# The end of the mix of a hybrid decoder layer: out gate by Tanh in block portions, norms of the linear group split by token halves

## What is computed

```python
x = x + 0.5 * swiglu(rmsnorm(x, g1), w_gate1, w_up1, w_down1)
h = rmsnorm(x, mix_norm)
sq, sk, sv, gq, gk, gv, gg, glr, mq = split(h @ w_in)
y_swa = swa_attention(sq, sk, sv, ...)        # sliding window of 128, 8 heads: 4 tiles of 128 rows
y_gla = gla(gq, gk, gv, gg, glr, ...)         # linear attention, 4 heads of 64: 2 tiles
#   inside: o = rmsnorm(o, norm_gain)  per head;  return o * silu(out_gate)
y_mem = memory_attention(mq, mk, mv, ...)     # cross attention into 256 memory tokens: 2 tiles
x = x + concat(y_swa, y_gla, y_mem) @ w_out
x = x + 0.5 * swiglu(rmsnorm(x, g2), w_gate2, w_up2, w_down2)
```

## Time and profile before

| | us |
|---|---|
| median of 3 runs | 1776.75 (1771.37 to 1780.1) |
| the profiled execution, its own time | 1777.78 |
| span of that execution in the trace | 1776.0 |
| mean granted TensorE clock in it | 0.988 of full |
| PE busy | 97% |
| DVE busy | 63% |
| ACT busy | 41% |
| POOL busy | 30% |

### The profile page before, as it was taken

How to read it: one execution, slowest core, us unless ns; L and a number is a source line. 1 busy time by engine, 2 the same in 40 slices (tenths; PEclk the granted TensorE clock), 3 DMA queues, 4 the chain that set the end, 5 groups by cost and what they waited for, 6 DMA issues and landing times.

```text
span 1776.0 us, 24794 instructions
## 1 busy us (share of the span) xinstructions
PE 1714.7 (97%) x8295; PEld 1389.5 (78%) x8295; DVE 1127.0 (63%) x1573; ACT 719.9 (41%) x1344; POOL 528.6 (30%) x432
## 2 busy tenths in 40 slices
PE   7999999999999999999999789999999999999999
PEld 4888888888778789877666568688888888877877
DVE  8965565555498684358788662896555555549654
ACT  5533333334234552142167721443333333334432
POOL 0444554443130231000056512044455444310000
PEclk9999999999999999999989989999999999999999
DMA  7142223324944330120100122113222332493334
GB/s 197 66 153 95 94 94 114 123 100 148 357 141 114 111 121 17 70 72 14 36 1 2 37 96 89 65 46 139 101 89 103 123 116 89 166 361 107 95 95 160
DMA packets 101693, 191.69 MB, mean 108 GB/s; under 512 B 11491, under 2 KB 13972, under 8 KB 101612
## 3 DMA queue, kind: packets, MB, share of 16 engines
q1 hardware_dynamic: 100528, 188.48, 31.3%
q0 software_dynamic: 848, 2.10, 0.9%
q10 hardware_dynamic: 236, 0.06, 0.0%
HBM read 139.74 MB, written 50.86 MB: 107 GB/s over the span
## 4 chain that ended last, share of the span: by engine, by line
PE 88%; DVE 3%; DMA 3%; ACT 2%; issue 1%; POOL 1%; SPq 1%; DVEq 0%; ACTq 0%; POOLq 0%
PE ps L56 27%; PE ps L57 27%; PE ps L58 27%; DMA down_raw<-act_dram 3%; PE ps L1565 1%; PE ps L1256 1%; POOL Pg L1883 1%; PE ps L1536 1%; ACT glu L1694 1%; DVE ps L1267 1%; PE ps L1517 1%; PE ps L2230 0%; SPq L971 0%; DVE p_lo L1188 0%; PE ps L1614 0%
## 5 line engine op out<-in xcount | busy, mean ns | idle before, releaser
L474 DVE TENSOR_TENSOR ring<-w_raw,ring 128x512 fp32r<-128x512 f32 x240 | 235.8, 997 | 220.2 <-ACT ring L469 220.0
L56 PE MATMUL ps<-hiT,ring 128*128 128x512 f32 x672 | 261.5, 389 | 0.0
L58 PE MATMUL ps<-hiT,ring 128*128 128x512 f32 x672 | 261.4, 389 | 0.0
L56 PE MATMUL ps<-down_ring 128*128 128x512 f32 x616 | 241.8, 392 | 11.2 <-DVE down_ring L847 6.9
L57 PE MATMUL ps<-loT,ring 128*128 128x512 f32 x640 | 249.0, 389 | 0.0
L57 PE MATMUL ps<-down_ring 128*128 128x512 f32 x616 | 239.9, 389 | 0.0
L58 PE MATMUL ps<-down_ring 128*128 128x512 f32 x616 | 239.8, 389 | 0.0
L56 PE MATMUL ps<-hiB,ring 128*128 128x512 f32 x576 | 225.7, 392 | 4.4 <-DVE loB L360 4.3
L58 PE MATMUL ps<-hiB,ring 128*128 128x512 f32 x576 | 224.6, 390 | 0.0
L469 ACT ACTIVATE ring<-w_raw 128x512 fp32r<-128x512 f32 x240 | 150.3, 628 | 175.7 <-PE ps L58 163.6
L847 DVE TENSOR_TENSOR down_ring<-down_raw,down_ring 128x512 fp32r<-128x512 f32 x176 | 126.4, 729 | 124.2 <-ACT down_ring L843 123.9
(11 more groups left out here) (242 smaller groups left out, 3020.2 us busy)
## 6 DMA issues: line engine op xcount, KB each, us to landing
down_raw<-act_dram SPq DMA_DIRECT2D x154, 256.0 KB, 2.6
w_raw<-in_w_gate SPq DMA_DIRECT2D x88, 256.0 KB, 3.1
w_raw<-in_w_up SPq DMA_DIRECT2D x88, 256.0 KB, 3.2
act_dram<-actT SPq DMA_DIRECT2D x88, 256.0 KB, 2.0
wd<-in_w_down SPq DMA_DIRECT2D x88, 256.0 KB, 5.4
act_dram<-act SPq DMA_DIRECT2D x66, 256.0 KB, 2.0
p_raw<-in_w_proj SPq DMA_DIRECT2D x15, 512.0 KB, 3.5
xT<-in_x SPq DMA_DIRECT2D x8, 512.0 KB, 7.4
```

The lines of the kernel that those rows point to most:

```text
L56: nc.tensor.matmul(out, w_hi, x_hi, start=first, stop=False, skip_group_check=resumed)
L58: return nc.tensor.matmul(out, w_lo, x_hi, start=False, stop=last, skip_group_check=resumed)
L474: nc.vector.tensor_tensor(ring[:, e % RING, 1, :], op_source(e), ring[:, e % RING, 0, :].bitcast(F32), ALU.subtract).then_inc(op_ready, 1)
```

## The change

In `mix_*` and `out_*`:

- The gate silu(z) = z * sigmoid(z) is computed as 0.5 * z * (1 + tanh(z / 2)). Per block ACT does a Tanh of 256 columns (`out_gate`) and DVE one instruction `(tanh + 1) * ggT` (`gate_out`), one block later; the factor 0.5 goes into the gain of the head norm. The one Silu over all tokens is gone.
- Pieces 0 and 1 (tokens 0 to 511) are squared by ACT in blocks 4 and 5, into a part of `qT` that is free by then, and not in block 7.
- In block 7 PE sums both pieces directly behind `turn(0, 7)`, after a wait for the memory exponentials, whose banks the sums use; `values(0, 7)` is moved ahead of `turn(2, 7)`.
- In block 7 ACT splits unit 19 and does the last Tanh and both roots ahead of `pt_copy(1, 7)`. DVE splits unit 19 straight behind `take_levels`, then does the last `gate_out`, the norm of piece 0, `swa_lo`, `mem_lo`.
- The first out group waits only for what its half of the tokens needs. PE does group 0's attention tiles, then the sums of pieces 2 and 3 together, then groups 1, 2, 3. The banks of the groups are shifted by two.
- DVE does the norms of pieces 1, 2, 3 behind unit 20, and unit 21 behind all of them.

```diff
+        tanh_of = place(87 * KB, ("tanh_of", [P, 2, P], F32))[0]
...
             if u == NPROJ:
                 dve.wait_ge(k_gated, NB)
+                dve.wait_ge(edge_ready, NB)
...
-            return {GLA_OUT: gla_squares[0][:, 0:w], GLA_OUT + 1: gla_squares[1][:, 0:w]}.get(i, glu[:, i % 2, 0:w])
+            return {GLA_OUT: qT[:, 0, 0:w], GLA_OUT + 1: qT[:, 1, 0:w]}.get(i, glu[:, i % 2, 0:w])
...
-            return ps[:, {GLA_OUT: 0, GLA_OUT + 1: 3}.get(i, 4 + i % 2), 0:w]
+            return ps[:, {GLA_OUT: 0, GLA_OUT + 1: 1}.get(i, 4 + i % 2), 0:w]
...
                 else:
+                    pe.wait_ge(probs_ready, probs_count(2, n))
                     head_sum(pe, GLA_OUT, HALF)
                     head_sum(pe, GLA_OUT + 1, HALF)
...
-                turn(2, n)
-                values(0, n)
+                    turn(2, n)
+                    values(0, n)
+                else:
+                    values(0, n)
+                    turn(2, n)
                 values(1, n)
                 mem_values(n)
+
+        FIRST_SQUARE_AT = (NB - 4, NB - 3)
...
+            def out_gate(n):
+                wait(act, out_gate_ready, n)
+                nc.scalar.activation(tanh_of[:], ggT[:, :, blk(n)], ACT.Tanh, scale=0.5).then_inc(out_gate_tanh, 1)
...
                 else:
-                    nc.scalar.activation(ggT[:], ggT[:], ACT.Silu).then_inc(out_gate_ready, 1)
-                    act.wait_ge(level_ready, NB - 1)
+                    unit_scalar(act, NPROJ)
+                    out_gate(n)
                     for c in range(2):
-                        head_square(act, GLA_OUT + c, gla_item(c)[2], HALF)
+                        head_root(act, GLA_OUT + c, HALF)
                 pt_copy(1, n)
                 o_copy(n)
                 if more:
                     exps(0, n + 1)
-                else:
-                    for c in range(2):
-                        head_root(act, GLA_OUT + c, HALF)
+                    out_gate(n)
                 pt_copy(2, n)
                 swa_hi(n)
-                if not more:
-                    unit_scalar(act, NPROJ)
+                if n in FIRST_SQUARE_AT:
+                    first_square(FIRST_SQUARE_AT.index(n))
                 mem_hi(n)
...
+            def gate_out(n):
+                dve.wait_ge(out_gate_tanh, n + 1)
+                nc.vector.scalar_tensor_tensor(out=ggT[:, :, blk(n)], in0=tanh_of[:], scalar=1.0, in1=ggT[:, :, blk(n)],
+                                               op0=ALU.add, op1=ALU.mult).then_inc(out_gate_ready, 1)
...
                 gate_edges(n)
+                if not more:
+                    gate_out(n - 1)
                 denominators(1, n)
                 take_levels(n)
...
                 if more:
+                    if n:
+                        gate_out(n - 1)
                     update_state(n)
...
                 else:
+                    unit_vector(dve, NPROJ)
+                    gate_out(n)
                     gla_norm(dve, 0)
                 swa_lo(n)
-                if not more:
-                    unit_vector(dve, NPROJ)
                 mem_lo(n)
...
-                else:
-                    gla_norm(dve, 1)
...
+                    if k == 0:
+                        pe.wait_ge(swa_lo_ready, NB // 2 * (h + 1))
                     if k == 6:
-                        pe.wait_ge(mem_y_lo_ready, NB)
+                        pe.wait_ge(mem_y_lo_ready, NB // 2 * (h + 1))
...
-            pe.wait_ge(swa_lo_ready, NB)
-            pe.wait_ge(head_normed, GLA_OUT + 1)
             for g in range(4):
-                if g == 3:
-                    pe.wait_ge(head_normed, GLA_OUT + 2)
+                if g in (2, 3):
+                    pe.wait_ge(head_normed, GLA_OUT + g - 1)
                 product(g, attention)
-                if g in (1, 2):
-                    head_sum(pe, GLA_OUT + g + 1, HALF)
+                if g == 0:
+                    pe.wait_ge(pt_ready, unit_count(2, NB - 1))
+                    head_sum(pe, GLA_OUT + 2, HALF)
+                    head_sum(pe, GLA_OUT + 3, HALF)
...
             dve.wait_ge(mem_y_lo_ready, NB)
             unit_vector(dve, NPROJ + 1)
+            gla_norm(dve, 1)
             gla_lo(dve, 0)
+            gla_norm(dve, 2)
             gla_lo(dve, 1)
-            gla_norm(dve, 2)
+            gla_norm(dve, 3)
+            gla_lo(dve, 2)
+            gla_lo(dve, 3)
             unit_vector(dve, NPROJ + 2)
-            gla_lo(dve, 2)
-            gla_norm(dve, 3)
-            gla_lo(dve, 3)
```

More of the change, by code:

```diff
@@ L1254, in head_sum @@
             pe.wait_ge(head_squared, i + 1)
-            wait(pe, head_normed, i - 1)
+            if i < GLA_OUT:
+                wait(pe, head_normed, i - 1)
             nc.tensor.matmul(head_bank(i, w), head_ones[:, :], head_buffer(i, w), start=True,
@@ L1705, in o_copy, with first_square @@
                                      ).then_inc(o_copied, 1)
+            def out_gate(n):
+                wait(act, out_gate_ready, n)
+                nc.scalar.activation(tanh_of[:], ggT[:, :, blk(n)], ACT.Tanh, scale=0.5).then_inc(out_gate_tanh, 1)
+            def first_square(c):
+                act.wait_ge(o_copied, NB // 2)
+                act.wait_ge(scored, unit_count(1, NB // 2 - 1))
+                head_square(act, GLA_OUT + c, gla_item(c)[2], HALF)
             def swa_hi(n):
@@ L1930, in gla_lo, with out_bank @@
                                     ALU.subtract).then_inc(gla_lo_ready, 1)
+        def out_bank(g):
+            return (g + 2) % 4
         def out_tensor(pe):
@@ L1944, in product @@
                     kc = slice(k * P, (k + 1) * P)
-                    mm = split_product(nc, ps[:, g % 4, :], p_hi[:, s, kc], p_lo[:, s, kc],
+                    mm = split_product(nc, ps[:, out_bank(g), :], p_hi[:, s, kc], p_lo[:, s, kc],
                                        hT_hi[:, k, cols], hT_lo[:, k, cols], k == 0, k == 5)
@@ L1972, in out_scalar @@
             root = lambda c: head_root(act, GLA_OUT + c, HALF)
+            unit_scalar(act, NPROJ + 1)
             act.wait_ge(o_copied, NB)
@@ L1976, in out_scalar @@
             gla_hi(act, 0)
-            unit_scalar(act, NPROJ + 1)
             root(2)
+            root(3)
+            unit_scalar(act, NPROJ + 2)
             gla_hi(act, 1)
-            unit_scalar(act, NPROJ + 2)
-            root(3)
             gla_hi(act, 2)
@@ L2013, in out_vector @@
                 dve.wait_ge(proj_ready, NG + i + 1)
-                nc.vector.tensor_tensor(part(xT, m, h), ps[:, g % 4, :], part(xT, m, h), ALU.add
+                nc.vector.tensor_tensor(part(xT, m, h), ps[:, out_bank(g), :], part(xT, m, h), ALU.add
                                         ).then_inc(out_added, 1)
@@ L2203, in _ @@
             dve.wait_ge(const_landed, 16 * NCONST)
-            for c in (0, 2):
-                nc.vector.tensor_scalar(head_gains[:, c:c + 1], head_gains[:, c:c + 1], float(HEAD) ** -0.5, None,
+            for c, by in ((0, float(HEAD) ** -0.5), (2, float(HEAD) ** -0.5), (4, 0.5)):
+                nc.vector.tensor_scalar(head_gains[:, c:c + 1], head_gains[:, c:c + 1], by, None,
                                         ALU.mult).then_inc(gains_scaled, 1)
@@ L2208, in _ @@
                                     ).then_inc(gains_scaled, 1)
-            dve.wait_ge(gains_scaled, 3)
+            dve.wait_ge(gains_scaled, 4)
             for m, h in norm_steps(1)[12:]:
```

9 lines of the change are left out of this document (4 added, 5 removed).

## The result

| | before | after |
|---|---|---|
| median, us | 1778.42 (4 runs, 1771.37 to 1780.15) | 1758.93 (4 runs, 1756.87 to 1759.67) |
| ratio | 1 | 0.9898, 95% interval 0.9881 to 0.9914 |
| profiled execution, us | 1777.78 | 1759.67 |
| span in the trace, us | 1776.0 | 1757.9 |
| mean granted clock | 0.988 | 0.992 |

What follows compares the result with a forecast made beforehand. PE, 97% busy, was the bound; four gaps and half clock around block 7 could give 20.0 us at most. Group 4 starting at 1037.2 instead of 1055.49, plus 0.4, made 18.6 us: 1758, range 1753 to 1765.

Steps and rivals of the forecast that it cites:

- What bounds: Block 7 to out group 4: four PE gaps, 12.9 us, plus 7.1 of half clock, 20.0 at most; gain 18.6.
- the stretch: Measure from the first matmul of block 7's levels to that of out group 4; 54.7 us before, 36.3 after.
- Head sums: Block 7, sums 0 and 1 right behind `turn(0, 7)`: 2 x 0.88 us at full clock, ending at 1005.8.
- The gap ahead of turn(1): Block 7: PE idle 1.4 us behind `take_levels` and `gate_out(6)`, taken as 0.6; the one gap left.
- turn(2): Block 7: moving `values(0, 7)` ahead just covers ACT's copy of unit 1; without that cover about 0.9 us.
- The 0.2 us ahead of `mem_values`: Block 7: small gap expected to stay, subtracted with the 1.4 from 20.0 in the cross check giving 18.4.
- Unit 19, group 0: Ahead of out group 0: `p_lo` done at 1008.4, 5 us before needed, so the 4.12 us gap is gone.
- DVE's race: Out groups: DVE's 18.0 us of work ends at 1033.1, linear part due at 1034.5, so 1.4 us cover.
- The loop: All blocks: added Tanh, squares and `gate_out` fit idle time, cost 0, 15.2 us per block; without cover 4.7.
- The clock: Block 7 to group 4: granted clock 1.00 throughout, with no window at half clock left.
- The 14% for a fall: Rival: clock still falls once, at the 1.4 us gap; costs 1.7 to 2.8 us, time 1760 to 1761; 14%.
- The slower rival: In 8 blocks Tanh and Exp evict each other's table: 2.3 us per block, 18.4 in all, 1776.5; 1.5%.

Runs made afterwards that it cites:

- the experiment with Sigmoid: Changed kernel with Sigmoid in place of Tanh and the gain's factor 0.5 made 1; 1778.34 us, ratio to the kernel before 1.0003.
- one Silu: Changed kernel with the gate of before: one Silu over all tokens in block 7 behind unit 19's split, no Tanh; 1764.63 us, ratio 0.9931.
- the further step: Changed kernel with each block's Tanh and product in the same block, block 7's Tanh in block 6, its product behind `mem_lo(7)`; 1760.74 and 1760.77 us.

## Why the prediction was right

The prediction was 1758, the measurement 1758.93. Point by point:

- **What bounds.** The gaps and the lower clock were named as worth 20.0 us at most, and 18.6 of it as the gain: 18.3 to the start of group 4 and 0.4 behind it. By the traces the stretch gave 18.4. Behind it the changed kernel was 1.1 us shorter, of which the 0.4 are a part. The changed kernel's mix began 1.4 us later, at 884.16 where the kernel before had 882.72; one difference ahead of it is the clock from 606 to 613 us, far from the change, which was 0.76 in the changed kernel's trace and 1.00 in the other's. In the second execution of the changed kernel the mix began at 885.10. The median of before came out 1.7 us higher with a fourth run. That the median of after lies within 1 us of the forecast is therefore in part luck: the intervals of the ratio allow a gain of 15 to 21 us. The stretch and its steps are what bears the prediction out.
- **Head sums.** Expected right behind `turn(0, 7)` at 0.88 each; they took 3.14 us less the gap of 1.25, 1.9 for both.
- **The gap ahead of turn(1).** Expected 1.4 for `gate_out(6)` of 0.6, measured 1.25. The instruction itself took 0.41, but the copies started 0.5 us later (1004.66 - 1003.26, the start of the product ahead of it, is 1.40; it was 0.88 in the earlier trace rows). The rest is the small addition behind it, which took 0.35 us where it had taken 0.15. What I had put at nothing is that POOL's scaling also suffered: `turn(0, 7)` waited 0.65 us for it and not 0.40. Both errors together are 0.1 us.
- **turn(2).** `values(0, 7)` was said to just cover the copy of unit 1. It did: the copy ended at 1011.47 and `turn(2, 7)` began at 1011.62 without a wait. The 0.2 us ahead of `mem_values` didn't come.
- **Unit 19, group 0.** No wait, as said.
- **DVE's race.** Expected cover of 1.4 us at the last `gla_lo`. It ended at 1034.54; PE reached the linear part of group 1 at 1014.82 + 84 x 0.227 + 1.75 = 1035.6, so 1.1. Close to the bound, and not beyond it.
- **The loop.** 0 was taken and found: 15.25 us per block over the last five, 15.27 before.
- **The clock.** At 1.00 through the whole stretch. The 14% for a fall were not too many: gaps of 1.35, 1.76, 1.94, 2.90 and 3.15 us in the variants had half clock behind them, while others of 1.36, 1.72 and 3.00 had not. The gap of 1.25 us that was left had none behind it in two executions.
- **On the clock of the earlier trace rows.** The changed trace runs 1.36 us behind the other at the levels of block 7. With that taken off, `turn(1, 7)` began at 1007.3 (1007.2 said), group 0 at 1013.5 (1013.7) and group 4 at 1037.1 (1037.2). The misses of 0.1 to 0.25 us partly cancel.
- **The slower rival** is the experiment with Sigmoid: priced at 2.3 us per block and 1776.5 without the clock, it took 2.23 per block and came to 1778, with one fall of the clock in the loop. Its condition, a load beside the gate, is what the built order excluded.

Undoing single parts costs 3.7 (Silu), 3.4 (low part of unit 19), 3.3 (out order), 1.1 (order of turn and values) and 1.0 (squares), 12.5 in all of the 18.4; of the first 1.2 and of the second 1.6 are half clock. Doing the gate alone gives 4.9, of which 3.4 lie in the clock's falls, and unit 19 alone 0.2. The parts don't add up, since each gap had several causes in a row and hid what came behind it. What I did not try is the release of group 0 for its half of the tokens by itself. An estimate from the changed trace: `swa_lo(7)` ended at 1015.46 and group 0 began at 1014.82, so with the old wait it would have started some 0.6 us later.

## What to carry to other kernels

At a seam between two phases, rebuild the timeline of every engine from the rows, instruction by instruction, and look at what is late next, before moving the instruction that a wait names: moving that one alone left the stretch at 54.55 us against 54.71. A function that shares its table with the one that runs anyway can be cut into portions and put into idle time for nothing; the same work with another table cost as much as the whole change gained. And a gap on TensorE costs more than its length when the clock falls behind it, here 1.2 to 2.8 us more, so a thin stretch is worth filling even with work that is needed only later. Before a total that fits is taken for a theory that holds, it is worth splitting it at one point in the middle: two of the totals here fitted because a shorter time at half clock made up for what the theory had wrong.

## What the runs showed of the hardware that I had not expected

POOL's scaling of unit 2 in block 7 took 2.89 us in the changed kernel. Its four instructions by duration (min, median, max in ns):

```profile
L1905 POOL TENSOR_SCALAR rstd<-rstd,row_inv x4: 473/474/1531, 1008.6 to 1011.0; 128x256 f32<-128x256 f32 x4
```

Three took 474 ns and one 1531, and beside it DVE ran the low part of unit 19 (1.19 us, two inputs in SBUF). In the variant that does this low part later, none took more than 484 ns, and POOL's timeline has

```profile
1004.01 1.85 POOL L1906 TENSOR_SCALAR rstd<-rstd,row_inv 128x256 f32<-128x256 f32 x4 [1.36 <-DVE row_inv L1797]
```

So the work that now stands beside it costs POOL 1.04 us, all of it in one instruction. `p_lo` is 0.80 of that: in the two kernels that have `p_lo` there but not the last `gate_out` behind it (one Silu, and the further step) the four took 2.65 us, one of them 1278 ns. The other 0.24 come with `gate_out(7)`, which follows `p_lo` at once. The Trainium skill (SBUF — State Buffer, "SBUF: two separate sides") says that the two engines share one pair of ports by an exclusive lock, taken by a VectorE instruction with two SBUF inputs for its whole length, and that the other engine then stands; this case agrees, with 0.80 us more on one GpSimd instruction beside a `p_lo` of 1.19 us that had begun 0.25 us earlier. POOL ended at 1011.51 and `turn(2, 7)` began at 1011.62: 0.1 us more and this would have been a wait of PE. The working of the prediction had no term for it.

The clock is not a function of the gap's length: 3.00 us of idle PE were followed by the 1.2 GHz level in the kernel before and with unit 19 alone, and by 1.00 throughout in the variant with the old out order and with the gate alone; 1.76 us were followed by a fall where 1.72 were not. The closest pair is in one execution: with Sigmoid, waits of 1.35 and 1.36 us at the same place of six blocks, between the same instructions, had the clock at 1.00 behind them five times and at 0.50 once.
